# Windowed attention of the second block: score and value matmuls by head halves of TensorE, and projections issued between the attention steps

## The reference, cut to what matters

```python
qkv = h @ w_qkv                                   # 1024 -> 1024 (q) + 128 (k) + 128 (v)
q = partial_rope(rmsnorm_2(q, q_gain), positions) # per head of 64
k = partial_rope(rmsnorm_2(k, k_gain), positions)
# per block of 128 queries, over the block before and its own:
s = jnp.einsum('bqkgd,bskd->bkgqs', qb, kb).astype(jnp.float32) * scale
s = jnp.where(valid, s, -jnp.inf)                 # 0 <= rel < 128
p = jax.nn.softmax(jnp.concatenate([s, sink_col], axis=-1), axis=-1)[..., :-1]
o = jnp.einsum('bkgqs,bskd->bqkgd', p.astype(vb.dtype), vb)
return out @ w_o                                  # 1024 -> 1024
```

## Time and profile before

| | |
|---|---|
| median of 3 runs | 1176.97 us (1176.05 to 1177.27) |
| profiled execution, its own time | 1178.79 us |
| its span, first to last instruction | 1177.1 us |
| TensorE busy | 98% of the span |
| VectorE, ScalarE, GpSimd busy | 72%, 55%, 6% |
| mean granted TensorE clock | 0.999 |

### The profile page before, as it was taken

The page is one execution under the profiler, slowest core; times in us unless marked ns, Lnnn a source line. Parts: engine busy times, 40 slices in busy tenths (PEclk is TensorE's granted clock), DMA queues, the critical chain, the costliest instruction groups (busy, mean ns, idle before and its releaser), DMA issues.

```text
span 1177.1 us, 16850 instructions
## 1 busy us (share of the span) xinstructions
PE 1147.9 (98%) x6614; PEld 992.9 (84%) x6614; DVE 845.9 (72%) x1324; ACT 650.8 (55%) x1083; POOL 65.8 (6%) x86
## 2 busy tenths in 40 slices
PE   5999999999999999999997999999999999999998
PEld 4888888899999888888875888888888988888887
DVE  5788976645556779998686678888777658677654
ACT  5554654556555465555466455555545775655551
POOL 1000000000001100400132010000020001000000
PEclk9999999999999999999999999999999999999999
DMA  8786983754445489999551347888737533677640
GB/s 301 279 293 230 345 288 143 282 191 172 143 164 176 148 321 330 353 338 317 180 180 40 108 178 253 311 294 314 272 139 295 198 107 118 228 243 249 237 160 36
DMA packets 42382, 263.50 MB, mean 224 GB/s; under 512 B 7360, under 2 KB 7744, under 8 KB 12480
## 3 DMA queue, kind: packets, MB, share of 16 engines
q1 hardware_dynamic: 42304, 262.42, 62.4%
HBM read 261.31 MB, written 1.10 MB: 223 GB/s over the span
## 4 chain that ended last, share of the span: by engine, by line
PE 89%; DVE 5%; ACT 3%; POOL 2%; issue 1%; DMA 1%; SPq 0%; POOLq 0%; DVEq 0%; ACTq 0%
PE ps L346 86%; DVE wl L982 2%; PE ps L535 1%; DMA raw<-in_stream 1%; PE ps L912 1%; ACT wh L1542 1%; PE ps L715 1%; DVE x L1017 0%; DVE xn L1087 0%; POOL small L1927 0%; ACT arena L1793 0%; POOL xn L1975 0%; DVE xn L1029 0%; PE ps L832 0%; POOL res L1933 0%
## 5 line engine op out<-in xcount | busy, mean ns | idle before, releaser
L982 DVE TENSOR_TENSOR wl<-raw,wh 128x1024 fp32r<-128x1024 f32 x374 | 450.1, 1224 | 32.3 <-ACT wh L1542 31.3
L346 PE MATMUL ps<-x,wh 128*128 128x512 f32 (+1 forms) x1984 | 445.3, 347 | 0.0
L1542 ACT ACTIVATE wh<-raw 128x1024 fp32r<-128x1024 f32 x374 | 388.7, 1051 | 46.9 <-PE ps L346 28.9
L346 PEld LDWEIGHTS ps<-x,wh 128*128 128x128 f32 x1984 | 342.4, 190 | 45.1 <-issue 3.4
L346 PE MATMUL ps<-x,wl 128*128 128x256 f32 x1568 | 264.7, 282 | 0.0
L346 PEld LDWEIGHTS ps<-x,wl 128*128 128x128 f32 x1568 | 236.7, 191 | 11.3
L346 PE MATMUL ps<-wh,x 128*128 128x512 f32 (+1 forms) x600 | 183.6, 384 | 2.3 <-DVE x L1017 2.1
L346 PE MATMUL ps<-wh,hh 128*128 128x512 f32 x404 | 158.9, 393 | 1.4 <-ACT arena L1850 1.4
L346 PE MATMUL ps<-wl,hh 128*128 128x512 f32 x404 | 157.9, 391 | 0.0
L346 PE MATMUL ps<-wh,hl 128*128 128x512 f32 x404 | 157.3, 389 | 0.0
L346 PEld LDWEIGHTS ps<-wh,x 128*128 128x128 f32 x600 | 111.8, 190 | 24.2 <-issue 1.9
(11 more groups left out here) (180 smaller groups left out, 846.6 us busy)
## 6 DMA issues: line engine op xcount, KB each, us to landing
raw<-in_stream SPq DMA_DIRECT2D x233, 1024.0 KB, 5.1
arena<-vectors SPq DMA_DIRECT2D x12, 512.0 KB, 6.2
arena<-in_tables SPq DMA_DIRECT2D x7, 576.0 KB, 5.9
raw<-in_stream SPq DMA_DIRECT2D x4, 512.0 KB, 9.4
gain_sb<-in_gains SPq DMA_DIRECT2D x3, 512.0 KB, 7.5
res<-in_x SPq DMA_DIRECT2D x4, 256.0 KB, 6.1
gain_sb<-in_c SPq DMA_DIRECT2D x2, 512.0 KB, 7.5
out_dram<-res SPq DMA_DIRECT2D x3, 256.0 KB, 2.0
```

The source lines that it names most:

```text
L346: return e.matmul(o, a, b, start=start, stop=stop)
L982: e.tensor_tensor(WL[:, n % NW, :], src, WH[:, n % NW, :].bitcast(F32), ALU.subtract).then_inc(*w_lo.tick(n))
L1542: e.activation(WH[:, m % NW, :], src, ACT.Copy).then_inc(*w_hi.tick(m))
```

## The change

All of it is in `sliding` of the four engines.

- **Scores**: `keys` is no longer a block matrix with zeros; for each of the two heads of a step TensorE issues one matmul that uses 64 of the array's rows, into bank 4 for the one head and bank 5 for the other. Both banks are claimed at every step.
- **Values**: V of one head is stationary (128x64, half of the array's columns), the transposed weights are moving (128 columns). The result comes out transposed, heads in the partitions, in banks 7, 2, 3, 7 for the four groups of four steps.
- **Sums**: since the values come out transposed, the inverse sums have to be as well. Per group, DVE spreads the eight inverses over 512 columns of `spread_out`, TensorE transposes that (`spread_sums`, four transposes), ACT copies it back to `spread_out`, DVE multiplies it by the values (`weighted`), and ACT and DVE split the product. `y_turn` goes away.
- **Transposed weights** all go through bank 6, where two banks took turns.
- **Order on TensorE**: `quarter(0)`, eight steps of tile 0, `move`, `quarter(1)`, eight steps of tile 0, eight of tile 1, the transposes of keys and first queries, then the 19 attention steps, with one or two projection steps behind each: first the last eight of `qkv2` for tile 1 (i = 0 to 7, beside the attention of tile 0), then the sixteen of `wo_a` for tile 0 (i = 8 to 18, beside the attention of tile 1). After that the sixteen of `wo_a` for tile 1, k = 0 to 3 for both halves, then k = 4 to 7, with `move(4, 0)` ahead of (k, c) = (6, 1).
- **Order on DVE and ACT**: the weight parts are made at other places, among the attention steps (DVE: eight of `wo_a` at i = 1, 2, 3, 6, 8, 10, 11, 12; ACT: six at i = 0, 1, 6, 8, 9, 10). `keys_turned(t)` and `keys_values(t)` are the old loop bodies made into functions. The four ACT copies of the normed rows (`res`) come after the weight parts. GpSimd no longer clears `KB`, and it turns tile 1's first heads before it takes the power for the second ones.

```diff
-    KB = AR(6528, 2 * S)
-    keys = KB.rearrange("p (h c) -> p h c", h=2)
+    keys = AR(6528, S)
-    y_at = {(0, 0): XN[1][0], (0, 1): XN[1][1], (1, 0): QK[1][:, 0:512], (1, 1): QK[1][:, 512:1024]}
+    spread_out = AR(ARENA + 5 * D, 512)
...
+    def window_scores(i, h):
+        return bank(4 + h, P * (i // 8 + 1))
+    Y_BANK = (7, 2, 3, 7)
...
-            turn = itertools.cycle([4, 5, 6, 7])
-            pair = []
+            pair = [take(("tq", "qkv2", i)) for i in range(2)]
+            for k in range(KT):
+                take(("tm", "qkv2", k))
...
+            def queries(k, t, c):
+                n = N["tm", "qkv2", k]
+                events = ([("qkv2", t, c)] if k == KT - 1 else []) + ([("used", n)] if (t, c) == (1, 1) else [])
+                token_major(n, x_side(q), k, t, c, k == 0, k == KT - 1, 0, *events)
+                if k == KT - 1:
+                    evicted[2 * t + c] = [vec.of("head", t, 8 * c)]
+            y_side = lambda k, t: (HH[:, k, P * t:P * t + P], HL[:, k, P * t:P * t + P],
+                                   x_hi.of("yw", t, k // 4), x_lo.of("yw", t, k // 4))
+            def outward(k, t, c):
+                n = N["tm", "wo_a", k]
+                events = ([("wo_a", t, c)] if k == KT - 1 else []) + ([("used", n)] if (t, c) == (1, 1) else [])
+                token_major(n, y_side, k, t, c, k == 0, k == KT - 1, 0, *events)
+                if k == KT - 1:
+                    evicted[2 * t + c] = [residual(4)(t, c)]
...
+            def scores(i):
+                t, m = i // 8, i % 8
+                pe.wait_ge(*acted.of("q", t, m // 4))
+                pe.wait_ge(*acted.of("k"))
+                claim(4)
+                claim(5)
+                for h in range(2):
+                    rows = slice(HD * h, HD * h + HD)
+                    z = mm(e, window_scores(i, h), QT[m][rows, P * t:P * t + P], keys[rows, 0:P * (t + 1)], True, True)
+                z.then_inc(*formed.tick(("scores", "w", i)))
+                evicted[4] = evicted[5] = [vec.of("low", "w", i, 1)]
+            def p_tiles(i):
+                claim(6)
+                pe.wait_ge(*acted.of("p", "w", i, 1))
+                for y in range(0, 2 * P * (i // 8 + 1), P):
+                    z = e.transpose(bank(6, P, y), SSC[i % 4][:, y:y + P], ident[:])
+                z.then_inc(*formed.tick(("p tiles", "w", i)))
+                evicted[6] = [(acted if i in COPIED_BY_ACT else vec).of("pt", "w", i)]
+            def values(i):
+                t, m = i // 8, i % 8
+                b = Y_BANK[i // 4]
+                if m % 4 == 0:
+                    claim(b)
+                pe.wait_ge(*(acted if i in COPIED_BY_ACT else vec).of("pt", "w", i))
+                for kt in range(t + 1):
+                    for h in range(2):
+                        at = P * ((t + 1) * h + kt)
+                        z = mm(e, bank(b, P, P * (m % 4))[HD * h:HD * h + HD, :], SV[kt][:, HD * h:HD * h + HD],
+                               SPT[i % 4][:, at:at + P], kt == 0, kt == t)
+                z.then_inc(*formed.tick(("values", "w", i)))
+                evicted[b] = [vec.of("y", "w", i // 4)]
+            def spread_sums(g, b):
+                claim(b)
+                place["spread", g] = b
+                pe.wait_ge(*vec.of("inverse", "w", g))
+                for j in range(4):
+                    z = e.transpose(bank(b, P, P * j), spread_out[:, P * j:P * j + P], ident[:])
+                z.then_inc(*formed.tick(("spread", g)))
+                evicted[b] = [acted.of("spread", g)]
+            quarter(0)
+            for k in range(4):
+                for c in range(2):
+                    queries(k, 0, c)
+            for half in range(2):
+                transposed(final_rows(q, 1)[half], vec.of("out", q, 1, half), 6 + half, "x", q, 1, half)
+                evicted[6 + half] = [x_lo.of("x", q, 1, half)]
+            quarter(1)
+            for ks in ((4, 5), (6, 7)):
+                for c in range(2):
+                    for k in ks:
+                        queries(k, 0, c)
+            for k in range(4):
+                for c in range(2):
+                    queries(k, 1, c)
+            turn_k()
+            turn_q(0, 0, 6)
+            for k in range(KT):
+                take(("tm", "wo_a", k))
+            for i in range(19):
...
+                    scores(i)
+                if i in (2, 7, 11):
+                    turn_q(*{2: (0, 1, 7), 7: (1, 0, 0), 11: (1, 1, 7)}[i])
+                if 2 <= i < 18:
+                    p_tiles(i - 2)
+                if i in (6, 10, 14, 18):
+                    spread_sums(i // 4 - 1, {6: 1, 10: 7, 14: 2, 18: 6}[i])
+                if i > 2:
+                    values(i - 3)
+                if i < 8:
+                    queries(4 + i % 4, 1, i // 4)
+                elif i < 12:
+                    for k in (2 * (i % 2), 2 * (i % 2) + 1):
+                        outward(k, 0, (i - 8) // 2)
+                elif i < 16:
+                    outward(i - 8, 0, 0)
+                else:
+                    for k in {16: (4, 5), 17: (6,), 18: (7,)}[i]:
+                        outward(k, 0, 1)
+            for ks in (range(4), range(4, KT)):
+                for c in range(2):
+                    for k in ks:
+                        if (k, c) == (6, 1):
+                            move(4, 0, itertools.cycle([4, 5]))
+                        outward(k, 1, c)
...
+            low_to(n + 6)
+            x_low(q, 1)
+            low_to(n + 7)
+            keys_turned(0)
+            low_to(n + 9)
+            keys_turned(1)
             scales(0, 0, 8, XN[0][0])
             scales(0, 8, 8, XN[0][1])
             turned_heads(0, 0, 8, bank(0), True)
-            scales(1, 0, 8, XN[1][0])
             turned_heads(0, 8, 8, bank(1), True)
-
-            def y_low(t, x):
+            n = N["tm", "wo_a", 0]
...
+            def weighted(g):
+                dv.wait_ge(*formed.of("values", "w", 4 * g + 3))
+                dv.wait_ge(*acted.of("spread", g))
+                e.tensor_tensor(spread_out, spread_out, bank(Y_BANK[g]), ALU.mult).then_inc(*vec.tick(("y", "w", g)))
             for i in range(19):
+                if i in (7, 11, 15):
+                    weighted(i // 4 - 1)
                 if i < 16:
...
+                if i in (5, 9, 13, 17):
+                    g = i // 4 - 1
+                    c = slice(8 * g, 8 * g + 8)
+                    dv.wait_ge(*acted.of("sink", g))
+                    dv.wait_ge(*acted.of("p", "w", 4 * g + 3, 1))
+                    e.tensor_tensor(total_w[:, c], total_w[:, c], extra_w[:, c], ALU.add).then_inc(*vec.tick(("total", g)))
+                    dv.wait_ge(*vec.of("total", g))
+                    inverse_of(total_w[:, c], inverse_w[:, c], "inverse sum", "w", g)
+                    if g:
+                        dv.wait_ge(*x_lo.of("yw", (g - 1) // 2, (g - 1) % 2))
+                    e.tensor_copy(heads(spread_out), inverse_w[:, c].unsqueeze(2).to_broadcast([P, 8, HD])).then_inc(
+                        *vec.tick(("inverse", "w", g)))
+                if i in (7, 11, 15):
+                    y_low(i // 4 - 1)
+                if i in (4, 8):
+                    scales(1, 2 * i - 8, 8, XN[1][i // 4 - 1])
+                if i in (5, 9):
+                    turned_heads(1, 2 * i - 10, 8, bank(2 + i // 8), False)
+                if i in (1, 2, 3, 6, 8, 10, 11, 12):
+                    low_to(n + (1, 2, 3, 6, 8, 10, 11, 12).index(i))
+            weighted(3)
+            y_low(3)
...
+            keys_values(0)
+            x_high(q, 1)
+            keys_values(1)
             e.preload_act_table_set("natural_log_exp_and_others")
+            high_to(n + 9)
+            for t in range(2):
+                for c in range(2):
+                    ac.wait_ge(*pooled.of("power", 3, t))
+                    ac.wait_ge(*vec.of("gained", 3, t, c))
+                    e.activation(RES[t][c], XN[t][c], ACT.Copy, scale=rstd[t][:, 0:1]).then_inc(*acted.tick(("res", t, c)))
             square_q(0, 0)
             square_q(0, 1)
+            n = N["tm", "wo_a", 0]
+            high_to(n + 1)
+            ac.wait_ge(*formed.of("turn k"))
+            e.activation(keys, bank(7, S), ACT.Copy, scale=k_scale).then_inc(*acted.tick(("k",)))
...
+                if i in (2, 7, 11):
+                    q_turned(*{2: (0, 1), 7: (1, 0), 11: (1, 1)}[i])
...
+                if i in (6, 10, 14, 18):
+                    sums_spread(i // 4 - 1)
+                if i in (7, 11, 15):
+                    y_high(i // 4 - 1)
+                if i in (4, 8):
+                    square_q(1, i // 4 - 1)
+                if i in (0, 1, 6, 8, 9, 10):
+                    high_to(n + 2 + (0, 1, 6, 8, 9, 10).index(i))
+            y_high(3)
```

More of the change, by code:

```diff
@@ L1814, in sliding @@
                     ac.wait_ge(*formed.of("p tiles", "w", j))
[L1815 to L1818 removed]
+                    if j > 3:
```

(4 more changed lines are left out.)

205 lines of the change are left out of this document (37 added, 168 removed).

## The result

The changed kernel takes 1181.95 us (median of 5 runs, 1180.8 to 1183.11) against 1176.9 for the kernel before (5 runs): ratio 1.0044, 95% interval 1.0029 to 1.0059. It is slower by 5.05 us; 3.0 were forecast, in a range of 1173.0 to 1184.5.

A forecast was written before the change was run, and what follows sets the result against it. TensorE, busy 98% of the span, was taken as the bound. Stage 92.85 against 91.5 us (+1.3), later transposes (+0.4) and half clock (+1.3) gave +3.0: 1180.0 us, range 1173 to 1184.5.

The forecast's parts named there:

- Exit: After the loop: tile 0's norm stands behind late weight parts, TensorE waits 5.4 us before `move(4, 0)`; `wo_a` ends after 17.35.
- Entry: Stage start to first scores: waits of 1.9 us on the sixth unit's low part and 1.7 on the next units' parts.
- The loop: The nineteen attention steps: 49.2 us, 8.4 of them waits, with three coupled queues each near full.
- TensorE's own work ... Sum 40.8: Nineteen attention steps: TensorE's work without waits, in blocks of 13.3, 21.7 and 5.8 us, 40.8 in sum.
- Together 5.4 us: Scores and values in array halves: TensorE saves 4.4 us in tile 1 and 1.0 in tile 0.
- The spread copy of DVE: DVE's four spreads of inverse sums: 0.69 us each, least known price; at double rate the loop about 1 us shorter.
- The clock: After the exit's long wait: a stretch at 1.2 GHz, 3.4 us long, costing 1.3 us net of slack.
- (1): Rival on the loop: attention hides better, the loop takes 42.5 us, total 1173.3; chance 0.20.
- (2): Rival at the exit: no wait before `move(4, 0)`; without it and the clock 1173.3 us; chance 0.06.
- (3): Rival on the clock: all as forecast, but it stays at 2.4 GHz, total 1178.7 us; chance 0.20.
- (4): Rival on the loop: head-of-line waits are worse, loop 55 us, total 1186; chance 0.10.
- (5): Rival on scores: halves do not overlap, scores take 0.43 and 0.92 again, 2.3 us more, total 1182; chance 0.04.

The follow-up runs named there:

- Used early: Changed kernel with the last sixteen projection steps unit by unit for k = 0 to 3 and DVE's three low parts in the norm's gaps: 1176.52 us.
- norm first: Changed kernel with DVE's three low parts of the next stage moved from ahead of tile 0's norm to behind it: 1179.02 us.
- values ahead of the transposes: Changed kernel with weight slots used earlier (1176.52 us), plus each step's values issued ahead of the transposes of weights: 1177.96 us.
- Short low parts: Changed kernel with DVE's low part of each of the eight `wo_a` units made for 128 of 1024 columns only: 1180.73 us.
- no fill: Changed kernel with all 24 projection steps taken out of the nineteen attention steps, eight before them and sixteen behind: 1198.65 us.
- scores alone: Kernel before, in its old order, with only the scores in row halves and both banks claimed at every step: 1177.58 us.

## Why the prediction was right, and what in it was not

The time, 1181.95, lies 2 above the forecast 1180.0 and in its range, and the sign is as forecast. By parts, counted from the stage's second matmul:

| | forecast | measured |
|---|---|---|
| to the first scores | 26.0 | 26.55 |
| the nineteen steps | 49.2 | 51.1 |
| of these, waits | 8.4 | 2.5 |
| gated product of tile 0 after the loop | 8.3 | 8.2 |
| transposes after the loop | 15.0 | 14.85 |
| the wait before them | 5.4 | 5.14 |
| end of `wo_a` after the loop | 17.35 and 1.3 of clock | 19.2 |

**Exit: right.** The wait has the place, the releaser and within 0.3 the length that were derived from the three `used` events, one high part and three low parts. "Used early" changes just these and the wait falls to 1.30; "norm first" shows that moving the low parts as a block only moves the wait.

**Entry: right.** 1.9 was forecast on the sixth unit's low part and 1.52 measured; 1.7 on the next units' parts, and 0.16 + 0.83 + 0.18 measured. The wait of 0.78 on the queries stands in the 0.7 that were set for them.

**The loop: right in its length, wrong in its make-up.** The step that failed is "TensorE's own work ... Sum 40.8" with, above it, "Together 5.4 us" saved. The prices of scores and values were right (0.42, 0.63, 0.37, 0.58). What was missing are the seams: about 5.6 us, by which the saving is eaten up. The other error has the opposite sign: 8.4 us of waits, measured 2.5. A TensorE that takes 5.6 longer arrives later at the same DVE and ACT results; "values ahead of the transposes" shows this, where 1.9 less of work came with 2.4 more of waits. But the places differ too: the 0.8, 1.3 and 0.8 before the scores of steps 8, 10 and 13 are absent, and the longest wait that did come, 1.34 for GpSimd at i = 7, isn't in the forecast. That the two errors cancel to within 2 us, and with them that the total came so near, is luck. "Short low parts" shows that DVE's load, counted as 38.7 us, was not close to the bound. Whether a TensorE without seams would have waited the whole 8.4 was not tested; "no fill" has a passage that stays at 48 us, but at a lower clock. The spread copy of DVE, the price left open, took 0.43:

```profile
629.00 0.43 DVE L1468 COPY arena<-small 128x512 f32<-128x512 f32 x1
```

That is about 1 us less in four than the 0.69 used. The Trainium skill ("VectorE: DVE Perf Modes", Mode 2×_2P), which lets a float32 copy inside SBUF run at double rate, agrees in direction: 0.43 against 0.69 is 1.6 times, though the 0.69 is of an instruction with a second operand, in PSUM.

**The clock: right that it falls, too small.** Forecast was 3.4 us at half rate, 1.3 net. It was 6.8 at the exit, of which 4.3 with work inside the stage, and 3.4 more in the loop behind a wait of only 1.34. This is the term that was mis-sized, in the profiled execution: counted by half it took 3.9 - 1.7 = 2.2 more than before inside the stage, and 0.9 beyond it (1.8 us at half rate), 3.1 in place of 1.3; by the pairs beside the table it is less, 2.1 to 2.7. The profiled pair differs by 6.4 up to the next transposes and the medians by 5.05; the mean granted clock of the five runs goes from 0.996 to 0.998, and the profiled one has the lowest, so part of the 6.4 is this execution's own. "Short low parts" has 0.997 in all six runs, and its profile shows the exit's 6.8 us at half rate alone; three of the changed kernel's five have the same 0.997, so the stretch in the loop is probably missing in them, and the clock's share in the median is nearer to the forecast than in the profile.

**The rivals.** (1), a loop of 42.5, fell: 51.1. (2), no wait before `move(4, 0)`, fell; with "norm first" it came true for that one place, and the time did not follow. (3), the clock stays up, fell in the changed kernel. (4), 55, fell. (5), halves that don't overlap, fell: 0.63 in tile 1, where it had 0.92 (in tile 0 its 0.43 can't be told from 0.42). Its total, 1182, is the nearest to the measured one all the same; that is chance.

Against the kernel before, then: waits 3.3 longer, and 2.2 for clock and own work together, by the table all of it clock, by the pairs 1.4 to 1.8 of it; that is the +5.5 of the profiled pair.

## What to carry to other kernels

Price a matmul by the distance to the next start in the order in which it will stand, not by its busy time among its like: each change between half-array shapes and work on the whole array cost 0.06 to 0.11 us, and at four changes a step they ate a saving of 5.4 us. When steps are moved, follow the slots that they free: here the wait that decided came from a weight buffer that was released after five projection steps where two would do, through ACT and DVE, to a norm that had nothing to do with it. Read the granted clock of every run, and not the time alone: work taken off TensorE can come back as half clock, as with "scores alone". And when work stands in the way of a norm, spread it over the gaps that the norm's own chain leaves; as one block it only moves the wait.

## What the runs showed of the hardware that was not expected

GpSimd and DVE hold each other up. The four products of 128x64 that turn tile 1's first heads, in the kernel before and in the changed one:

```profile
629.64 1.15 POOL L1994 TENSOR_TENSOR arena<-arena 128x64 f32<-128x64 f32 x4
```

```profile
630.63 2.15 POOL L2037 TENSOR_TENSOR arena<-arena 128x64 f32<-128x64 f32 x4 [0.80 <-DVE arena L1385]
```

In the first case DVE read out of PSUM beside them; in the second it made a low part, out of two operands in SBUF, and that took its usual time:

```profile
631.34 1.26 DVE L1023 TENSOR_TENSOR wl<-raw,wh 128x1024 fp32r<-128x1024 f32 x1
```

"Short low parts" is the test of it: there this low part is made for 128 columns alone and takes 0.32, and the same four products take 1.20:

```profile
632.03 1.20 POOL L2039 TENSOR_TENSOR arena<-arena 128x64 f32<-128x64 f32 x4 [0.80 <-DVE arena L1387]
```

It also goes the other way. With units used early GpSimd began an addition first, and the low part that began 0.56 later took 1.81:

```profile
669.52 1.29 POOL L1985 TENSOR_TENSOR res<-res,xn 128x512 f32<-128x512 f32 x1 [23.85 <-DVE xn L1072]
```

```profile
670.08 1.81 DVE L1025 TENSOR_TENSOR wl<-raw,wh 128x1024 fp32r<-128x1024 f32 x1 [0.64 <-ACT wh L1596]
```

The Trainium skill ("GPSIMD Engine Reference", Key points) says that GpSimd shares its SBUF interfaces with VectorE and contends with instructions that read two SBUF inputs; the trace agrees, at 1.0 us for the products and 0.6 for the low part. The 1.0 lies in the chain that TensorE waits 1.34 for at i = 7, and with the short low part that wait is 0.40. That run shortened all eight low parts, but the 0.9 that the products gained are the 0.9 that the wait lost.

And a wait of 1.34 us was followed by a stretch at 1.2 GHz in the changed kernel, while one of 1.33 at the same place, with units used early, was not; in "scores alone" a stretch of 6.8 us began behind waits of 0.86 and 0.33. The length of the wait alone doesn't tell.
